# A hybrid decoder trunk on one core: the experts' up and gather products in four 32-column matmuls instead of one of 128

## The chip, the cores and the metric

The kernel runs on 1 core of one Trainium2 chip. The metric is the device time of one launch in microseconds (us); the kernel before takes 1231.05 us, the median of 3 runs (1229.32 to 1233.52).

## The reference, cut to what matters

Two layers over 256 tokens of 1024 features, all in float32. Each layer mixes the tokens in four groups of heads (sliding-window attention, gated linear attention, stick-breaking attention, RWKV-7), projects, adds, normalises, and applies a feed-forward part: dense in layer 0, and in layer 1 a mixture of 8 experts of which each token takes two. Only that mixture is touched by the change:

```python
def swiglu(h, w1, w3, w2):
    return (jax.nn.silu(h @ w1) * (h @ w3)) @ w2

def moe_swiglu(h, router, w1, w3, w2):
    logits = (h @ router).astype(F32)
    top_vals, top_idx = lax.top_k(logits, TOP_K)
    gates = jax.nn.softmax(top_vals, axis=-1)
    combine = jnp.sum(jax.nn.one_hot(top_idx, N_EXPERTS, dtype=F32) * gates[..., None], axis=-2)
    out = jnp.zeros_like(h)
    for e in range(N_EXPERTS):
        out = out + combine[..., e:e + 1].astype(h.dtype) * swiglu(h, w1[e], w3[e], w2[e])
    return out
```

w1 and w3 of an expert are 1024 x 1408, w2 is 1408 x 1024: 17.3 MB for each expert.

## The kernel before, in words

The kernel is written engine by engine (`build`, from line 196): one block of code for each of SyncE (SP, which issues the weight transfers), TensorE (`pe`), ScalarE (`act`), GpSimd and VectorE (`dve`). Each runs its own list in the order in which it is written; they meet through semaphores only: `full[b]` counts how often PSUM bank b was filled by TensorE, `free[b]` how often it was emptied. The order of the work is written by hand.

Layer 0 and the mixers of layer 1 come first. Then the function `experts` (called at the end of the `pe` block) does the mixture. The router picks experts; VectorE makes of the choice a one-hot matrix `pick` of 256 tokens x 96 slots (CAP = 96) for one expert. Then a loop of 8 passes runs on all engines (`Fori(0, n_passes * N_EXPERTS)`, where n_passes is 1 for these inputs), one pass per expert. One pass on TensorE is, in this order:

- **Up** (L1021 to L1035): 11 chunks of 128 hidden features. For each chunk and each of w1 and w3, 8 matmuls accumulate over the 1024 input features: the stationary operand is a 128x128 block of weights, the moving one the 96 gathered tokens (`slot_h`, in `region_m`). Chunks alternate between bank 0 and bank 1. After each chunk ScalarE applies silu (L1313) and VectorE multiplies (L1405, a helper), which frees the bank.
- **Transposes** (L1040) of the 96 weighing columns for this expert.
- **Gather** (`gather`, L994 to L1005) for the next expert: 8 feature blocks x 2 token tiles, the stationary operand a 128x128 block of normalised tokens in `tok`, the moving one `pick` with 96 columns, into banks 6 and 7. A first gather stands ahead of the loop.
- **Down** (L1047 to L1062): 22 matmuls of 512 columns whose stationary operand is 128 x 96 activations and whose moving one is w2, into banks 2 and 3 (96 partitions).
- **Scatter** (L1064 to L1069): 4 matmuls of 512 columns, `weigh_t` times `slot_y`, added to `x_sb` by VectorE.

All matmuls go through the helper `mm` (L517). Each float32 matmul of the program appears in the trace as two LDWEIGHTS (load of the stationary operand, PEld) and two MATMUL records; transposes (L522, L828, L1040) as one of each. One pass is 438 pairs of a load and a MATMUL: 352 in up, 2 transposes, 32 in the gather, 44 in down and 8 in the scatter.

SyncE loads each expert in 18 pieces (6 pairs of w1 and w3 columns, 6 pieces of w2; 1 MB each, the last of each kind half), into a ring of 9 slots, six in `ring` and three in `region_e`. Piece k + 9 is asked for when piece k has been used: for the up pieces the wait is on `full[0]` or `full[1]` after the second chunk of the pair.

Elsewhere the program has products on a part of the array: `GAT` in `b_scores` writes 64 partitions at a time, four matmuls of 64 weight columns and 256 moving columns, alternately to partitions 0 to 63 and 64 to 127 of one bank; `LW` and `LA` in `layer_mixers` contract over 64 rows, LW over rows 0 to 63, LA over rows 64 to 127, two matmuls each.

Of the kernel before, what the change touches and what calls it, by code (L numbers as in the profile page):

```python
# [11 lines left out]
AX_X = mybir.AxisListType.X  # L12

P = 128
D = 1024
KC = D // P
SEQ = 256
NT = SEQ // P
DEPTH = 2
# [12 lines left out]
D_FFE = 1408  # L32
UPC = D_FFE // P
UP2 = (UPC + 1) // 2
# [17 lines left out]
CAP = 96  # L52
# [31 lines left out]
def shape_constants():  # L84

    t = np.zeros((P, N_CONST), np.float32)
    i = np.arange(P)[:, None]
    j = np.arange(P)[None, :]

# [103 lines left out]
def build(nc, t_in, out):  # L193
    ctx = ExitStack()
    with ctx:
        def sb(name, shape, dt=F32):
            return ctx.enter_context(nc.sbuf_tensor(name, shape, dt))


        x_sb = sb("x_sb", [P, NT, D])  # L200
        tok = sb("tok", [P, NT, D])
        hT = sb("hT", [P, KC, SEQ])
# [21 lines left out]
        banks = [ctx.enter_context(nc.psum_tensor(f"bank{i}", [P, 512], F32)) for i in range(8)]  # L224
# [85 lines left out]
        slot_h = region_m[:, 0:KC * CAP].rearrange("p (c s) -> p c s", c=KC)  # L310
        pick = region_m[:, 768:768 + NT * CAP].rearrange("p (t s) -> p t s", t=NT)
        weigh = region_m[:, 960:960 + NT * CAP].rearrange("p (t s) -> p t s", t=NT)
        weigh_t = region_m[0:CAP, 1152:1152 + SEQ].rearrange("p (t n) -> p t n", t=NT)
        slot_y = region_m[0:CAP, 1408:1408 + D]
        place = region_m[:, 2432:2432 + NT * W].rearrange("p (t i) -> p t i", t=NT)
# [33 lines left out]
        def bank(name, l):  # L349
            return banks[uses[name, l][0]]  # L350
# [11 lines left out]
        def wait_open(pe, name, l):  # L362

            b, n = uses[name, l]
            if n:
                pe.wait_ge(free[b], n)
# [11 lines left out]
        def slot(n):  # L378
            return n % SLOTS
# [40 lines left out]
        def _(sp):  # L420
# [31 lines left out]
            for n, (what, l, at, m) in enumerate(pieces):  # L452
# [4 lines left out]
                elif n == 2:  # L457
                    sp.wait_ge(landed[slot(0)], 16)
                size = (KC if what in ("w_in", "w1", "w3") else D) * m
                dst = ring[:, slot(n), 0:size].rearrange("p (c n) -> p c n", n=m if size == KC * m and what not in ("w_out", "w2") else D)  # L460
                sp.dma_start(dst, source(what, l, at, m)).then_inc(landed[slot(n)], 16)
# [53 lines left out]
        def _(pe):  # L515
            def mm(o, lhsT, rhs, start=False, stop=False):
                return nc.tensor.matmul(o, lhsT, rhs, start=start, stop=stop, skip_group_check=True)  # L517
# [20 lines left out]
            def wait_features(names, l, k):  # L538

                if names and k % 2 == 0:  # L540
                    wait_evacuated(pe, names[k // 2], l)
# [432 lines left out]
            def experts(l):  # L974
                wait_open(pe, "RT", l)
                for t in range(NT):
                    for k in range(KC):
                        if t == 0:
                            wait_features(("F0", "F1", "F2", "F3"), l, k)
                        last = mm(bank("RT", l)[:, t * N_EXPERTS:(t + 1) * N_EXPERTS], hT[:, k, t * P:(t + 1) * P],  # L980
                                  router_sb[:, k, :], start=(t == 0 and k == 0), stop=(k == KC - 1))
                fills(last, "RT", l)


                pe.wait_ge(sem("chosen_ready"), 1)
                wait_open(pe, "POS", l)
                o = bank("POS", l)
                before, sel = const("upper")[:, 0:P], (chosen[:, 0, 0:N_EXPERTS], chosen[:, 1, 0:N_EXPERTS])
                mm(o[:, 0:8], before, sel[0], start=True, stop=True)
                mm(o[:, 8:16], const("all"), sel[0])  # L990
                mm(o[:, 8:16], before, sel[1], stop=True)
                mm(o[:, 16:24], const("all"), sel[0])
                fills(mm(o[:, 16:24], const("all"), sel[1], stop=True), "POS", l)

                def gather(b, waits):

                    for h in range(2):
                        if waits is not None:
                            pe.wait_ge(free[6 + h], waits[h])
                        for c in range(4):  # L1000
                            for t in range(NT):
                                last = mm(banks[6 + h][:, c * CAP:(c + 1) * CAP],
                                          tok[:, t, (4 * h + c) * P:(4 * h + c + 1) * P], pick[:, t, :],
                                          start=(c == 0 and t == 0), stop=(t == NT - 1))
                        last.then_inc(full[6 + h], 1)  # L1005

                pe.wait_ge(sem("picks"), 1)
                wait_open(pe, "G0", l)
                wait_open(pe, "G1", l)
                gather(0, None)  # L1010

                def landed_piece(i, k):
                    s, n = expert_landed(i, k)
                    pe.wait_ge(s, n)

                pe.wait_ge(sem("passes_ready"), 1)
                n_passes = pe.value_load(passes_i[0:1, 0:1], min_val=1, max_val=MAX_PASSES)
                with pe.Fori(0, n_passes * N_EXPERTS) as i:
                    pe.wait_ge(free[6], nth(i, 6, 0))
                    pe.wait_ge(free[7], nth(i, 7, 0))  # L1020
                    for p2 in range(UP2):  # L1021
                        m = min(256, D_FFE - 256 * p2)
                        landed_piece(i, 2 * p2)
                        landed_piece(i, 2 * p2 + 1)
                        w1 = expert_slot(2 * p2, KC * m).rearrange("p (c n) -> p c n", c=KC)
                        w3 = expert_slot(2 * p2 + 1, KC * m).rearrange("p (c n) -> p c n", c=KC)
                        for jj in range(m // P):
                            j = 2 * p2 + jj
                            b = j % 2
                            pe.wait_ge(free[b], nth(i, b, j // 2))  # L1030
                            for f, w in enumerate((w1, w3)):
                                for k in range(KC):
                                    last = mm(banks[b][:, f * CAP:(f + 1) * CAP], w[:, k, jj * P:(jj + 1) * P],
                                              slot_h[:, k, :], start=(f == 0 and k == 0), stop=(k == KC - 1))
                            last.then_inc(full[b], 1)  # L1035

                    pe.wait_ge(sem("weighs"), i + 1)
                    pe.wait_ge(free[2], nth(i, 2, 0))
                    for t in range(NT):
                        last = nc.tensor.transpose(banks[2][0:CAP, t * P:(t + 1) * P], weigh[:, t, :], ident)  # L1040
                    last.then_inc(full[2], 1)

                    pe.wait_ge(sem("picks"), i + 2)
                    gather(i, (nth(i, 6, 0), nth(i, 7, 0)))
                    pe.wait_ge(free[2], nth(i, 2, 1))
                    pe.wait_ge(free[3], nth(i, 3, 0))
                    for k2 in range(UP2):  # L1047
                        m = min(2, UPC - 2 * k2)
                        landed_piece(i, 2 * UP2 + k2)
                        w = expert_slot(2 * UP2 + k2, m * D).rearrange("p (c n) -> p c n", c=m)  # L1050
                        for kk in range(m):
                            j = 2 * k2 + kk
                            pe.wait_ge(free[j % 2], nth(i, j % 2, j // 2 + 1))
                        for half in range(2):
                            for kk in range(m):
                                k = 2 * k2 + kk
                                last = mm(banks[2 + half][0:CAP, :], slot_act[:, k, :],
                                          w[:, kk, half * 512:(half + 1) * 512], start=(k == 0), stop=(k == UPC - 1))
                            if k2 == UP2 - 1:
                                last.then_inc(full[2 + half], 1)  # L1060
                        if k2 < UP2 - 1:
                            last.then_inc(sem("moe_w2_used"), 1)  # L1062

                    for q, (b, t, half) in enumerate(SCATTER):  # L1064
                        pe.wait_ge(free[2 + half], nth(i, 2 + half, 2 - half))
                        if b > 3:
                            pe.wait_ge(free[b], nth(i, b, 0))
                        mm(banks[b][:, :], weigh_t[:, t, :], slot_y[:, half * 512:(half + 1) * 512],
                           start=True, stop=True).then_inc(full[b], 1)  # L1069
# [864 lines left out]
```

## Time and profile before

| | |
|---|---|
| median of 3 runs | 1231.05 us (1229.32 to 1233.52) |
| span of the profiled execution | 1229.1 us |
| the 8 passes of the expert loop | about 525 us of it |
| TensorE busy (MATMUL) | 1190.4 us, 97% |
| TensorE weight loads busy | 929.9 us, 76% |
| VectorE, ScalarE, GpSimd busy | 285.9, 192.3, 60.8 us |
| chain that ended last | TensorE 95%, VectorE 3% |
| transfers | 213.29 MB, mean 174 GB/s |

The span is measured from the first to the last instruction of that execution; no time of its own beside the span is recorded for the profiled execution, and the median of the runs is 1.95 us above it. How to read it: a MATMUL's duration holds its way through the array, so durations overlap, and what one costs in a row of them is the distance from one start to the next: the start of a group, its length and its count give it.

### The profile page before, as it was taken

Reading aid. Unit: us, or ns where it says so; the run is one execution under the profiler, and the core shown is the slowest. Engines: PE = TensorE matmul, PEld = TensorE weight load, DVE = VectorE, ACT = ScalarE, POOL = GpSimd, SP = SyncE. Lnnn points to the kernel's source line nnn. Section 1 sums busy time; section 2 is a strip of 40 time slices with the busy share of each in tenths; the row PEclk is TensorE's granted clock in tenths of the full one; section 3 lists DMA queues with packets and bytes.
Section 4 is the critical chain, followed back from the end, with each engine's and each line's share of the span. In section 5 each row is a group of like instructions: output and inputs, shape, how many; then the busy total and the mean of one; then the engine's idle time right before and its main releaser. Section 6 shows DMA issues by size and latency. Waiting matters only on the chain.

```text
span 1229.1 us, 16224 instructions
## 1 busy us (share of the span) xinstructions
PE 1190.4 (97%) x6686; PEld 929.9 (76%) x6686; DVE 285.9 (23%) x645; ACT 192.3 (16%) x444; POOL 60.8 (5%) x67
## 2 busy tenths in 40 slices
PE   7999999999999999999998899999999999999996
PEld 6886895688886448878884795959596978878692
DVE  4332663200000013143744201010110201010102
ACT  2243230200000002342221110010100101000011
POOL 2002221000000000004010000000000000000000
PEclk8999999899999999999999799999999999999998
DMA  9542102355445453432014378796969696878850
GB/s 326 166 137 69 35 2 70 100 172 169 137 137 196 146 154 120 139 103 69 1 35 152 108 269 259 257 306 227 305 204 318 214 306 219 301 232 289 253 205 34
DMA packets 168647, 213.29 MB, mean 174 GB/s; under 512 B 5120, under 2 KB 151200, under 8 KB 168480
## 3 DMA queue, kind: packets, MB, share of 16 engines
q1 hardware_dynamic: 166032, 210.29, 52.3%
q10 hardware_dynamic: 2576, 2.45, 0.7%
q8 instruction: 29, 0.48, 0.2%
q14 instruction: 10, 0.08, 0.0%
HBM read 211.67 MB, written 1.05 MB: 173 GB/s over the span
## 4 chain that ended last, share of the span: by engine, by line
PE 95%; DVE 3%; issue 1%; ACT 1%; POOL 0%; DMA 0%; DVEq 0%; POOLq 0%; ACTq 0%
PE bank L517 93%; PE bank L522 1%; DVE tok L1429 1%; POOL small L1338 0%; DMA x_sb<-in_x 0%; DVE b_att L1611 0%; DVE b_q L1408 0%; DVE x_sb L1405 0%; DVE region_m L1405 0%; PE bank L828 0%; ACT tok L1116 0%; DVE small L1420 0%; PE bank L1040 0%; ACT hT L1128 0%; PE bank L796 0%
## 5 line engine op out<-in xcount | busy, mean ns | idle before, releaser
L517 PE MATMUL bank<-hT,ring 128*128 128x256 f32 (+1 forms) x1184 | 261.8, 383 | 0.0
L517 PEld LDWEIGHTS bank<-hT,ring 128*128 128x128 f32 (+1 forms) x1184 | 224.4, 190 | 36.7 <-issue 2.9
L517 PEld LDWEIGHTS bank<-region_m,ring 128*128 128x128 f32 x2048 | 232.8, 193 | 5.1 <-issue 5.1
L517 PE MATMUL bank<-region_m,ring 128*128 128x96 f32 x2048 | 234.1, 276 | 1.6 <-DVE region_m L1855 1.6
L517 PE MATMUL bank<-ring,region_e 128*96 128x512 f32 (+1 forms) x368 | 159.4, 592 | 0.0
L517 PEld LDWEIGHTS bank<-ring,region_e 128*96 128x96 f32 (+1 forms) x368 | 64.1, 176 | 88.5 <-issue 88.5
L1405 DVE TENSOR_TENSOR region_e<-region_f,bank 128x96 f32<-128x96 f32 (+1 forms) x110 | 31.6, 287 | 424.4 <-ACT region_f L1313 279.8
L517 PE MATMUL bank<-ring,hT 128*128 128x256 f32 (+1 forms) x448 | 127.8, 442 | 1.4 <-ACT hT L1133 1.4
L517 PE MATMUL bank<-region_e 128*128 128x128 f32 (+2 forms) x512 | 117.7, 380 | 0.0
L517 PEld LDWEIGHTS bank<-ring,hT 128*128 128x128 f32 x448 | 84.0, 190 | 35.7 <-issue 25.8
L517 PEld LDWEIGHTS bank<-region_e 128*128 128x128 f32 (+1 forms) x512 | 70.4, 187 | 46.8 <-issue 46.7
L517 PE MATMUL bank<-region_m,region_e 128*128 128x96 f32 x768 | 88.4, 275 | 0.0
L517 PEld LDWEIGHTS bank<-region_m,region_e 128*128 128x128 f32 x768 | 87.0, 192 | 0.0
L1313 ACT ACTIVATE region_f<-bank 128x96 f32<-128x96 f32 x88 | 22.0, 250 | 315.5 <-PE bank L517 315.5
L1338 POOL TENSOR_TENSOR small<-small 128x1 f32<-128x1 f32 (+1 forms) x18 | 18.6, 1033 | 887.9 <-DVE small L1420 826.1
L1405 DVE TENSOR_TENSOR x_sb<-x_sb,bank 128x512 f32<-128x512 f32 x44 | 30.3, 688 | 93.5 <-PE bank L517 93.5
L517 PE MATMUL bank<-region_f 128*128 128x128 f32 (+1 forms) x352 | 43.0, 275 | 0.0
L517 PEld LDWEIGHTS bank<-region_f 128*128 128x128 f32 x352 | 41.2, 192 | 1.6 <-issue 1.6
L1875 DVE COPY region_m<-bank 96x512 f32<-96x512 f32 x8 | 5.5, 687 | 143.1 <-PE bank L517 143.1
L517 PE MATMUL bank<-region_m,tok 128*128 128x96 f32 x288 | 35.4, 284 | 1.2 <-DVE region_m L1778 1.2
L517 PEld LDWEIGHTS bank<-region_m,tok 128*128 128x128 f32 x288 | 34.8, 201 | 1.3 <-DVE region_m L1778 1.3
L522 PE MATMUL bank<-consts,tok 128*128 128x128 f32 x96 | 16.9, 325 | 14.1 <-DVE tok L1429 14.1
(234 smaller groups left out, 702.1 us busy)
## 6 DMA issues: line engine op xcount, KB each, us to landing
ring<-in_moe_w SPq DMA_DIRECT2D x80, 1024.0 KB, 6.0
region_e<-in_moe_w SPq DMA_DIRECT2D x40, 1024.0 KB, 5.7
ring<-in_ffn_w SPq DMA_DIRECT2D x33, 1024.0 KB, 5.4
ring<-in_w_in SPq DMA_DIRECT2D x22, 1024.0 KB, 5.3
ring<-in_w_out SPq DMA_DIRECT2D x8, 1024.0 KB, 4.9
ring<-in_moe_w SPq DMA_DIRECT2D x16, 512.0 KB, 5.3
region_e<-in_moe_w SPq DMA_DIRECT2D x8, 512.0 KB, 3.4
ring<-in_w_in SPq DMA_DIRECT2D x2, 1088.0 KB, 5.5
```

The source lines that it names most:

```text
L517: return nc.tensor.matmul(o, lhsT, rhs, start=start, stop=stop, skip_group_check=True)
L522: last = nc.tensor.transpose(bank(name, l)[:, cc * 256 + t * P:cc * 256 + t * P + P], tok[:, t, (2 * c2 + cc) * P:(2 * c2 + cc + 1) * P], ...
L1313: nc.scalar.activation(slot_silu[:, b, :], banks[b][:, 0:CAP], ACT.Silu).then_inc(sem("moe_silu"), 1)
L1338: g.tensor_tensor(ap_out, ap_in, m_half[:, 0:n], ALU.pow).then_inc(sem("rstd_ready"), 1)
L1405: return v.tensor_tensor(o, a, b, op)
L1429: v.tensor_scalar(tok[:, t, s], x_sb[:, t, s], scale, None, ALU.mult).then_inc(sem("h_ready"), 1)
L1875: v.tensor_copy(slot_y[:, 512:1024], banks[3][0:CAP, :]).then_inc(free[3], 1)
```

## The change

`HALF = 32` is a new constant. In the gather and in the up products, each matmul with 128 stationary columns and 128 output partitions becomes four, each with 32 stationary columns, which write partitions 0 to 31, 32 to 63, 64 to 95 and 96 to 127 of the same bank. The moving operand of all four is the same 96 columns. Nothing else changes; the new constant's line moves the lines behind it by one, the two new loops those behind them by more.

```diff
 P = 128
+HALF = 32
 D = 1024
...
                         for c in range(4):
                             for t in range(NT):
-                                last = mm(banks[6 + h][:, c * CAP:(c + 1) * CAP],
-                                          tok[:, t, (4 * h + c) * P:(4 * h + c + 1) * P], pick[:, t, :],
-                                          start=(c == 0 and t == 0), stop=(t == NT - 1))
+                                for q in range(0, P, HALF):
+                                    at = (4 * h + c) * P + q
+                                    last = mm(banks[6 + h][q:q + HALF, c * CAP:(c + 1) * CAP],
+                                              tok[:, t, at:at + HALF], pick[:, t, :],
+                                              start=(c == 0 and t == 0), stop=(t == NT - 1))
                         last.then_inc(full[6 + h], 1)
...
                             for f, w in enumerate((w1, w3)):
                                 for k in range(KC):
-                                    last = mm(banks[b][:, f * CAP:(f + 1) * CAP], w[:, k, jj * P:(jj + 1) * P],
-                                              slot_h[:, k, :], start=(f == 0 and k == 0), stop=(k == KC - 1))
+                                    for q in range(0, P, HALF):
+                                        at = jj * P + q
+                                        last = mm(banks[b][q:q + HALF, f * CAP:(f + 1) * CAP], w[:, k, at:at + HALF],
+                                                  slot_h[:, k, :], start=(f == 0 and k == 0), stop=(k == KC - 1))
                             last.then_inc(full[b], 1)
```

TensorE's list at the head of the loop, before: the wait for the two pieces, then one chunk, 16 matmuls into all 128 partitions (two trace pairs each).

```order
L1018 ISA
L1014 ISA
L1014 REGISTER_ALU
L1030 ISA
L517 MATMUL bank<-region_m,ring 128x96 x16
L1030 ISA
L517 MATMUL bank<-region_m,ring 128x96 x16
```

The same place in the changed kernel:

```order
L1021 ISA
L1017 ISA
L1017 REGISTER_ALU
L1033 ISA
L518 MATMUL bank<-region_m,ring 32x96 x64
L1033 ISA
L518 MATMUL bank<-region_m,ring 32x96 x64
```

A chunk is now 64 matmuls into 32 partitions each; the waits between chunks stay where they were.

The end of the pass, before: last chunk, transposes, gather, first part of down.

```order
L517 MATMUL bank<-region_m,ring 128x96 x16
L1037 REGISTER_ALU
L1038 ISA
L1040 MATMUL bank<-consts,region_m 96x128 x2
L1043 REGISTER_ALU
L517 MATMUL bank<-region_m,tok 128x96 x16
L1045 REGISTER_ALU
L1046 ISA
L517 MATMUL bank<-ring,region_e 96x512 x12
```

And in the changed kernel:

```order
L518 MATMUL bank<-region_m,ring 32x96 x64
L1042 REGISTER_ALU
L1043 ISA
L1045 MATMUL bank<-consts,region_m 96x128 x2
L1048 REGISTER_ALU
L518 MATMUL bank<-region_m,tok 32x96 x64
L1050 REGISTER_ALU
L1051 ISA
L518 MATMUL bank<-ring,region_e 96x512 x12
```

No instruction has changed its place; between two runs of 32-partition matmuls stand the transposes, and behind the gather the 96-partition matmuls of down.

## Rows read from the trace of the kernel before

**Rows 1.** The page: span, engines, and the chain by line.
```profile
span 1229.1 us, 16224 instructions
PE 1190.4 (97%) x6686; PEld 929.9 (76%) x6686; DVE 285.9 (23%) x645; ACT 192.3 (16%) x444; POOL 60.8 (5%) x67
PE 95%; DVE 3%; issue 1%; ACT 1%; POOL 0%; DMA 0%; DVEq 0%; POOLq 0%; ACTq 0%
```

**Rows 2.** The chain in order of time, pieces of the loop: start us, us, what.
```profile
734.00 65.41 PE bank L517 x436
...
865.25 65.40 PE bank L517 x436
...
1127.74 65.41 PE bank L517 x436
```

**Rows 3.** TensorE's timeline, one pass: start us, us, engine line op out<-in xcount.
```profile
825.59 21.58 PE L517 MATMUL bank<-region_m,ring 128*128 128x96 f32 x192
847.00 9.10 PE L517 MATMUL bank<-region_m,region_e 128*128 128x96 f32 x80
855.94 1.95 PE L517 MATMUL bank<-region_m,ring 128*128 128x96 f32 x16
857.72 1.95 PE L517 MATMUL bank<-region_m,region_e 128*128 128x96 f32 x16
859.51 5.52 PE L517 MATMUL bank<-region_m,ring 128*128 128x96 f32 x48
864.87 0.38 PE L1040 MATMUL bank<-consts,region_m 128*96 128x128 f32 x2
865.09 3.71 PE L517 MATMUL bank<-region_m,tok 128*128 128x96 f32 x32
...
887.57 3.80 PE L517 MATMUL bank<-region_m 96*128 96x512 f32 x8
```

**Rows 4.** The same view, long runs of 256 and of 512 moving columns.
```profile
239.83 60.38 PE L517 MATMUL bank<-hT,ring 128*128 128x256 f32 x279
...
385.50 64.97 PE L517 MATMUL bank<-ring,region_e 128*128 128x512 f32 x151
```

**Rows 5.** The timeline around GAT, then the durations and starts of its eight MATMULs.
```profile
133.72 0.44 PE L707 MATMUL bank<-consts,hT 128*128 128x128 f32 x2
134.09 0.63 PEld L517 LDWEIGHTS bank<-b_q,hT 128*64 128x64 f32 x8 [0.17 <-issue]
134.09 1.08 PE L517 MATMUL bank<-b_q,hT 128*64 128x256 f32 x8
135.10 0.60 PE L517 MATMUL bank<-region_e 128*128 128x128 f32 x3
...
L517 PE MATMUL bank<-b_q,hT x8: 379/379/431, 134.1 to 134.8; 128*64 128x256 f32 x8
...
134.09 0.14 PEld L517 LDWEIGHTS bank<-b_q,hT 128*64 128x64 f32 x2 [0.17 <-issue]
```

**Rows 6.** The timeline at LW (rows 0 to 63) and LA (64 to 127).
```profile
39.13 0.18 PEld L517 LDWEIGHTS bank<-region_m,lora 64*128 64x128 f32 x1 [0.33 <-issue]
...
39.15 0.18 PEld L517 LDWEIGHTS bank<-region_e,lora 64*128 64x128 f32 x1
```

**Rows 7.** Stretches: PE, PEld, DVE, ACT, POOL busy, PEclk, DMA share, GB/s.
```profile
762.00:769.00 7.00, 7.00 (x66) 7.00 (x64) 1.21 (x5) 0.50 (x2) 0.00 (x0) 1.00 0.15 43
...
804.00:811.00 7.00, 7.00 (x18) 2.64 (x17) 0.20 (x1) 0.00 (x0) 0.00 (x0) 1.00 1.02 312
...
825.60:891.20 65.60, 65.60 (x439) 51.59 (x438) 8.25 (x25) 5.98 (x18) 0.00 (x0) 1.00 0.79 264
```

**Rows 8.** Queues (packets, MB, share): whole page; 692 to 745 us; 745 us to 1193 us.
```profile
q8 instruction: 29, 0.48, 0.2%
...
q8 instruction: 4, 0.07, 0.5%
...
q14 instruction: 1, 0.01, 0.0%
```

**Rows 9.** Waits, 745 us to the end of the passes: waiter <- waited for: us, times, longest.
```profile
ACT region_f L1313 <- PE bank L517: 272.8, 76, 6.2
DVE region_e L1405 <- ACT region_f L1313: 238.5, 76, 3.3
```

**Rows 10.** The first gather, before the loop, and the stretch with its granted clock.
```profile
685.31 5.74 PE L517 MATMUL bank<-region_m,tok 128*128 128x96 f32 x32 [1.19 <-DVE region_m L1778]
...
681.00:689.00 8.00, 6.00 (x27) 5.90 (x28) 3.67 (x28) 0.31 (x2) 0.00 (x0) 0.50 0.01 2
```

**Rows 11.** Transfer issues of one pass: KB each, median us from issue to landing.
```profile
ring<-in_moe_w SPq DMA_DIRECT2D x10, 1024.0 KB, 6.0
```

## The prediction

> **What bounds the kernel now.** I read the page first: TensorE is busy for 97% of the span and has 95% of the chain that ended last; the chain knows no transfer to speak of [rows 1]. The chain in order of time then shows the loop of experts as eight equal pieces of 65.4 us, about 65.6 us from one to the next (734.00 to 1127.74 in six steps), unbroken TensorE work [rows 2]. So each nanosecond that a matmul of the loop gives back shortens the span, until something else is late. The loop is 525 us of the 1229.1.
>
> TensorE's timeline of one pass tells what a matmul costs there. From 825.59 to 859.51 stand 192 + 80 + 16 + 16 = 304 MATMULs of 96 moving columns, 33.92 us, so one starts every 111.6 ns [rows 3]. That is not the time in which 96 columns stream. Long runs of wider matmuls give that: 279 of 256 columns in 60.38 us are 216.4 ns each, 151 of 512 columns in 64.97 us are 430.3 ns each [rows 4]. The difference, 213.9 ns for 256 columns, is 0.836 ns a column, and 2.5 ns are left over for each matmul. For 96 columns this makes 80.2 + 2.5 = 82.7 ns. What takes 111.6 ns must be the load of 128 weight columns: at the same 0.836 ns a column it is 107 ns, plus 4.6. With 256 columns the load is hidden behind the stream, with 96 the stream is hidden behind the load. **Up and gather are bound by weight loads**, and the change cuts each load to a quarter, at the price of four times as many loads and four times as many streams. Everything hangs on whether the four streams run side by side.
>
> **Do parts of the array run side by side?** The kernel before has a place that shows it for halves. GAT's matmuls use 64 weight columns each and write alternately to the lower and the upper 64 partitions. Its eight MATMULs of 256 columns all start between 134.1 and 134.8 us and take 1.08 us from first start to last end [rows 5]; one after the other, their starts alone would be spread over 7 x 216 = 1.51 us. The first two loads lie in one piece of 0.14 us, which is the length of a single one [rows 5]. So two column tiles both load and stream at the same time, each at its full rate, though both belong to float32 matmuls and read all 128 rows. A second place shows that the queue lets work of another tile past: LW issues four loads and four MATMULs before LA's first load in program order, yet LA's first load starts at 39.15, 0.02 us behind LW's first [rows 6]. In the changed kernel the next tile's work stands only four instructions behind. Eight instructions in at most 0.03 us (by the two printed digits) are under 4 ns each; a group of four 32-column matmuls has four loads and four MATMULs per step of 82.7 ns, 10.3 ns each. Four tiles at once, and such a rate kept up for 30 us, no row shows.
>
> **The change part by part.**
>
> - *Up and gather in the loop.* Of each pass 352 + 32 = 384 pairs become 4 x 384. If four tiles stream side by side, a group of four starts every 82.7 ns in place of one every 111.6: 28.9 ns for each old pair, 11.1 us a pass, times 8: **-88.8 us**. A tile's own load, at 32 x 0.836 + 4.6 = 31.4 ns, hides behind its own stream of 82.7. The bounds of the group's period: 80.2 (no leftover at all) and 4 x 82.7 = 330.8 (no overlap at all). I take 82.7, by GAT, whose streams were not slowed by being two.
> - *The first gather.* It stands ahead of the loop, 32 pairs in 5.74 us, partly while the granted clock is 0.50, the 1.2 GHz level [rows 10]: 179 ns each. The same share, 26% of it, is **-1.5 us**.
> - *Going into small tiles and out again.* Around GAT: the transpose before it starts last at 133.72 + 0.44 - 0.27 = 133.89, and GAT at 134.09 where 0.11 later was due: 0.09 lost. Its last start is 134.8, 0.71 behind the first for three steps of two, where 0.65 was due: 0.06. The next matmul starts at 135.10, 0.30 later for 0.22: 0.08. The three behind take 0.60 with the last's 0.27 in it, 0.33 for two steps in place of 0.22: 0.11 [rows 5]. Together 0.34 us there and back. A pass does it twice (up, then the transposes, then the gather), the program 17 times: **+5.8 us**; nothing to double of that is the bound.
> - *Instruction fetches.* The trace has 29 of 0.48 MB in all, 16.5 KB each; four in the first pass, and in the seven others none but one small one of another queue [rows 8]: the loop is fetched once and stays. The program has (6686 - 7 x 438) x 2 = 7240 loads and MATMULs to fetch, so 66 bytes each. The loop grows from 876 to 2 x (1536 + 54) = 3180 of them, 0.21 MB or 13 fetches. Whether that much stays is not shown. If it does, nothing is added. If not, 13 fetches come back in every pass. One lasts 0.5% of 16 x 53 us / 4 = 1.06 us [rows 8], and a group of 256 instructions is used up in 2.6 us, so fetching ahead keeps up; straight code does so now without a gap (60.38 us of TensorE without an idle moment [rows 4]). What can show is the jump back, where nothing was fetched ahead: 1.06 us, behind scatter's 3.80 us of queued matmuls [rows 3]. Between 0 and two fetches a pass (17 us) I take half of one, since most of the first should be covered: **+4 us**. The Trainium skill, page "Runtime: NRT & Kernel Launch", section "Instruction fetch mechanics", gives TensorE's memory as 2048 instructions and says that a branch to a page which is not there waits for its fetch. By it the old loop fits and the new one does not, and these fetches will be seen; that no fetch stands in the seven later passes agrees for the old one.
> - *Everything else.* ScalarE waits 272.8 us for TensorE behind up chunks and VectorE 238.5 us for ScalarE [rows 9]; a chunk of 32 groups lasts 2.65 us in place of 3.57, two banks alternate, and both still wait. Nothing to add. Down and scatter are unchanged.
> - *The weights.* They hide behind TensorE; the cover shrinks from 65.6 to 65.6 - 11.1 + 0.7 = 55.2 us a pass. The transfers of a pass kept all engines busy for 0.79 of 65.6 us, 51.8 us [rows 7]. That still fits, with 3.4 us to spare. The share has been 1.02 over 7 us, and between bursts 0.15, when SyncE waited for a slot [rows 7]. Half a pass lies between asking and needing, against a median of 6.0 us to land [rows 11]. So 0, but it is the next thing to be late.
>
> Sum: -88.8 - 1.5 + 5.8 + 4 = -80.5 us, from the profiled 1229.1 to 1148.6. The runs shown lie 1.95 us above that execution in the median, so **1150.5 us**. This case's own range: 1136 (no leftover per matmul, 7.5 us; no fetch seen, 4; and some rounding) to 1167 (switches twice as dear, two fetches shown in each pass).
>
> **The rivals.**
>
> - *The weights become the bound.* For it: 51.8 us of transfers in a pass of 55.2 is 0.94 of all engines, which the old pass never sustained because of the waits for slots between bursts. Against: the lead of half a pass smooths bursts. At a share of 0.88 a pass lasts 58.9 us, 6.7 less than now: 8 x 6.7 = 54, so 1176.
> - *A floor on each matmul's issue.* GAT's pairs start within 0.01 us, but there were eight. If every MATMUL took 25 ns of issue, a group would take 100 ns, 11.6 less than now: 36 us less 10 for switches and fetches, 1205. The Trainium skill states just this number: page "TensorE: Matmul & The Clock Gate", section "Wait — 56ns, not 53.3ns?", says that start-to-start never falls below about 25 ns however few the columns. By that rule the sum would be 1205 and not 1150; starts of two tiles in one 0.14 us piece [rows 5] speak for counting it per tile.
> - *Instructions come too slowly*, the case on the other side. If the 13 fetches of a pass were not fetched ahead, each would stop TensorE for 1.06 us: 104 of them cost 110 us, more than the 90.3 gained, so 1231 - 90 + 6 + 110 = 1257. It decides from 0.8 us shown per fetch. Against it: straight code hides them now, at a slower use.
> - *Loads of different tiles queue for one path.* Then a group takes 4 x 31.4 = 125.6 ns, or 117 if only 2.5 ns are lost per load, against 111.6 now: 1258 to 1285. The one pair of loads in 0.14 us speaks against it.
> - *Only two tiles stream at a time.* All that the trace shows is two. A group then takes 2 x 82.7 = 165.4 ns, 53.8 more than now, on 3104 old pairs: +167, with switches and fetches 1408.
>
> **How the numbers follow.** Chances: the forecast 0.62, weights 0.10, issue floor 0.07, instructions 0.05, loads in line 0.06, two at a time 0.10. About 0.3%, 3.7 us, is what a measurement can tell from no change. Faster: 0.62 + 0.10 + 0.07 = 0.79, of which I move 0.01 to no change, where a mixture of cases could land; slower 0.21. Up to 1210 the cases hold under 0.79, less the tails of the first; so the range goes on to 1260, which takes in the instructions and the cheaper end of the loads: 1136 to 1260.
>
> **What would show it.** Right: TensorE's timeline with 128 MATMULs of 32x96 every 2.65 us, passes 55 to 56 us apart in the chain, SyncE waiting less, DMA share near 0.93. The weights: TensorE idle ahead of a piece, released by a transfer. The issue floor: passes near 62 us with TensorE never waiting. Fetches: 13 packets of the instruction queue in each pass, and TensorE idle at the head of the loop. Two at a time or loads in line: passes of 86 or 68 us, the starts of the four tiles spread over 165 or 117 ns. The forecast is wrong if a pass is longer than 58 us.

## The result and the profile after

| | before | after |
|---|---|---|
| median of 4 runs | 1230.18 us (1228.49 to 1233.52) | 1363.45 us (1354.62 to 1367.33) |
| span of the profiled execution | 1229.1 us | 1365.5 us |
| mean granted clock of TensorE | 0.982 | 0.939 |
| ratio of the times | | 1.1071, 95% interval 1.1035 to 1.1108 |

The change makes the kernel 10.7% slower, 133 us; 1150.5 us was forecast. The page of the changed kernel: span, busy time, the granted clock in 40 slices, the instruction queue, the chain by engine, and the groups of the 32-column matmuls.

```profile
span 1365.5 us, 34848 instructions
PE 1170.9 (86%) x15998; PEld 888.0 (65%) x15998; DVE 285.9 (21%) x645; ACT 192.9 (14%) x444; POOL 60.9 (4%) x67
PEclk9999999999999999999889999899998889989898
q8 instruction: 137, 2.24, 0.7%
PE 84%; issue 12%; DVE 2%; ACT 1%; POOL 0%; DMA 0%; DVEq 0%; POOLq 0%; ACTq 0%
L518 PE MATMUL bank<-region_m,ring 128*32 128x96 f32 x8192 | 224.1, 276 | 89.1 <-issue 87.5
L518 PE MATMUL bank<-region_m,region_e 128*32 128x96 f32 x3072 | 83.5, 266 | 52.2 <-issue 52.2
L518 PE MATMUL bank<-region_m,tok 128*32 128x96 f32 x1152 | 30.5, 265 | 17.2 <-issue 16.0
```

TensorE was busy for 97% and had 95% of the chain [rows 1]; now it is busy for 86%, and 12% of the chain is "issue": the engine had nothing to run and waited for nothing that the profile shows. No DMA and no other engine took its place. The loss stands ahead of the new matmuls (89.1 + 52.2 + 17.2 us). The packets of the instruction queue went from 29 [rows 8] to 137.

The chain in order of time, one pass in the middle of the loop (start us, us, what), says where:

```profile
998.43 24.97 PE bank L518 x149
1023.40 3.09 issue
...
1029.53 10.46 PE bank L518 x382
1039.98 3.29 issue
1043.28 7.13 PE bank L518 x254
1050.41 2.50 issue
1052.91 2.84 PE bank L518 x127
1056.76 2.85 PE bank L518 x127
1059.60 3.83 issue
1063.43 10.53 PE bank L518 x381
...
1082.80 24.97 PE bank L518 x149
```

Before, this was one piece of 65.4 us [rows 2]. Now 84.4 us lie from one down product (998.43) to the next (1082.80). In between are bursts of about 127, or two or three times that, and pauses of 2 to 4 us. 128 MATMULs with their loads are 256 instructions. By the page a packet of the instruction queue is 2.24 MB / 137 = 16.4 KB, and at the 66 bytes each of the prediction that is about 250 instructions: **one packet, one burst**. The first piece, 24.97 us, is down, scatter and the first matmuls of the next pass; then follows the pause at the jump back, 3.09 us here and 3.2 and 3.7 in its neighbours. The queues in 520 us of the loop:

```profile
q1 hardware_dynamic: 86251, 105.53, 61.7%
q8 instruction: 86, 1.41, 1.1%
```

Before, seven of the eight passes had none of these packets [rows 8]. In the records of the trace 111 stand behind the loop's start, 14 a pass, 3.0 us apart at the least, 4.3 in the median, up to 7.6 in up and gather; one lasts 1.05 us.

The jump itself is on record as an instruction of TensorE's queue. Here it is before and after: the shortest, the median and the longest duration in ns, of eight (the shortest, the last pass's, jumps nowhere).

```profile
L1018 PEldq COMPARE_BRANCH  x8: 76/208/248, 757.5 to 1216.8; - x8
L1021 PEldq COMPARE_BRANCH  x8: 83/5612/7128, 765.9 to 1353.2; - x8
```

Where the loop is fetched anew, the jump takes 5.2 to 7.1 us in place of 0.2. The next packet of the instruction queue starts 2.7 to 4.6 us behind the jump's start and lasts 1.1 us, and the jump ends some 1.4 us behind it. So one fetch that is waited for takes over 5 us, of which the packet is one; scatter's queued matmuls cover part of it.

Inside a burst the array did what was forecast: 127 MATMULs end after 2.84 us, and the last one's 0.24 us taken off, this is 82 to 83 ns for each group of four (82.7 forecast). Often the four tiles of a group start 7 ns apart; elsewhere they are out of step, at the same 82 to 83 ns a group.

The granted clock adds its share. Two stretches of 10 us (busy us of PE, PEld, DVE, ACT, POOL; then PEclk, DMA share, GB/s):

```profile
860.00:870.00 10.00, 9.10 (x296) 8.76 (x292) 0.51 (x2) 0.50 (x2) 0.00 (x0) 0.65 0.01 3
890.00:900.00 10.00, 6.42 (x289) 5.77 (x280) 0.76 (x3) 0.72 (x3) 0.00 (x0) 1.00 0.93 363
```

At 890 TensorE is idle for a third of the time at full clock, and as many MATMULs (289 against 296) are done as at 860, where it is busy for 91% at a mean clock of 0.65. Over the loop the clock stands at 0.50, the 1.2 GHz level, for 126 us; before it was 3.4 us. A group of four takes 160 ns there, so a stretch at half clock eats up part of the time in which the next block arrives; clock and pauses can't simply be added.

### The profile page after: what moved, and what is told of

Read it like the earlier page. It is cut to its first block, busy times and chain, and to the rows that moved or that the text cites. A ratio compares the mean times of both kernels' runs of the same rounds, so it can differ in the third digit from the quotient of the medians.

```text
span 1365.5 us, 34848 instructions
## 1 busy us (share of the span) xinstructions
PE 1170.9 (86%) x15998; PEld 888.0 (65%) x15998; DVE 285.9 (21%) x645; ACT 192.9 (14%) x444; POOL 60.9 (4%) x67
## 3 DMA queue, kind: packets, MB, share of 16 engines
q8 instruction: 137, 2.24, 0.7%
HBM read 211.67 MB, written 1.05 MB: 156 GB/s over the span
## 4 chain that ended last, share of the span: by engine, by line
PE 84%; issue 12%; DVE 2%; ACT 1%; POOL 0%; DMA 0%; DVEq 0%; POOLq 0%; ACTq 0%
PE bank L518 82%; PE bank L523 1%; DVE tok L1434 1%; POOL small L1343 0%; DMA x_sb<-in_x 0%; DVE b_att L1616 0%; DVE b_q L1413 0%; PE bank L1045 0%; DVE x_sb L1410 0%; DVE region_m L1410 0%; PE bank L829 0%; ACT tok L1121 0%; DVE small L1425 0%; ACT hT L1133 0%; PE bank L797 0%
## 5 line engine op out<-in xcount | busy, mean ns | idle before, releaser
L518 PE MATMUL bank<-region_m,ring 128*32 128x96 f32 x8192 | 224.1, 276 | 89.1 <-issue 87.5
L518 PEld LDWEIGHTS bank<-region_m,ring 128*32 128x32 f32 x8192 | 211.2, 126 | 103.6 <-issue 103.5
L518 PE MATMUL bank<-region_m,region_e 128*32 128x96 f32 x3072 | 83.5, 266 | 52.2 <-issue 52.2
L518 PEld LDWEIGHTS bank<-region_m,region_e 128*32 128x32 f32 x3072 | 76.1, 121 | 57.4 <-issue 57.4
L518 PE MATMUL bank<-region_m,tok 128*32 128x96 f32 x1152 | 30.5, 265 | 17.2 <-issue 16.0
L518 PEld LDWEIGHTS bank<-region_m,tok 128*32 128x32 f32 x1152 | 27.0, 119 | 20.4 <-issue 19.1
L518 PE MATMUL bank<-region_m 96*128 96x512 f32 x64 | 30.4, 617 | 0.0
```

## The experiments

Two readings stood against each other. **A, supply**: the loop has grown from 919 to 3223 instructions (loads, MATMULs and 43 others), no longer stays with the engine and is fetched anew in every pass, more slowly than it is used up. **B, the array**: four narrow tiles cost something in themselves, say in the clock, and the fetches only go along. A loop "stays" if passes behind the first bring no packets of the instruction queue. A block is 256 instructions, about what one packet holds. Each ratio is to the kernel before, run beside the experiment on the same chip.

**Half the instructions, nearly the same gain on the array.** `e1_two64` changes one number of the changed kernel:

```diff
-HALF = 32
+HALF = 64
```

> Up and gather in two matmuls of 64 weight columns in place of four of 32. Theory (the instruction supply is what failed: the loop of 3180 loads and MATMULs no longer stays and its blocks of 256 come slower than they are used): here the loop has 2 x (768 + 54) = 1644. If that stays, two tiles side by side give the same period of 82.7 ns as four, no instruction fetch after the first pass, and the sum of the prediction without its fetch term: 1229.1 - 88.8 - 1.5 + 5.8 + 2 = about 1147 us. If 1644 do not stay, fetches come back, 6 or 7 a pass, but a block then lasts 5.3 us of streaming, so 1150 to 1180. Rival (small column tiles themselves stall the engine, whatever the instructions): slower than before, 1260 to 1300 by half of the loss.

Measured 1143.84 us (1141.67 to 1145.25), ratio 0.9298 (0.9272 to 0.9325). The chain in order of time:

```profile
943.05 54.73 PE bank L518 x820
997.78 0.35 PE bank L1045 x2
998.13 54.73 PE bank L518 x820
```

The passes are unbroken again and last 55.08 us, where the forecast for the changed kernel had 55.2. Behind 745 us the instruction queue of TensorE has no packet at all. The expectation was about 1147. So two tiles side by side give what the sum said; B in its plain form ("split products don't pay") is gone.

**Four tiles, few instructions.** `e2_gather32` undoes the split of up and keeps that of the gather:

```diff
+                            n = P
...
-                                    for q in range(0, P, HALF):
+                                    for q in range(0, P, n):
...
-                                        last = mm(banks[b][q:q + HALF, f * CAP:(f + 1) * CAP], w[:, k, at:at + HALF],
+                                        last = mm(banks[b][q:q + n, f * CAP:(f + 1) * CAP], w[:, k, at:at + n],
```

> Only the gather in four matmuls of 32 columns, up as before. Theory: 2 x 534 = 1068 instructions in the loop stay resident, no fetch after the first pass; 9 gathers of 32 pairs gain 28.9 ns each, 8.3 us, less 9 x 0.34 = 3.1 for going into small tiles and out: about 5 us faster than before, 1225 us. Rival (four tiles stall by themselves): each gather longer than 3.7 us, so slower than before by 5 us or more.

Measured 1223.59 us (1220.99 to 1224.4), ratio 0.9948 (0.993 to 0.9967): 6.4 us gained, about as expected (1225). Four narrow tiles are no loss where the loop (1111 instructions) stays: 4 packets behind its start, all in the first pass.

**How long may the loop be?** `e3_up32_5` and `e5_up32_4` leave the gather whole and split the first 5 or 4 of the 11 chunks of up into four; the edit of the second:

```diff
+                            n = HALF if j < 4 else P
...
-                                    for q in range(0, P, HALF):
+                                    for q in range(0, P, n):
```

> Up in four matmuls of 32 columns for chunks 0 to 4 of 11, the other chunks and the gather as before: 2 x (438 + 480) = 1836 loads and MATMULs in the loop. Theory (supply) with a memory of some 2000 instructions: stays, 160 old pairs a pass gain 28.9 ns, 37 us in all, less 8 x 0.34 = 2.7: about 1196 us, and no fetches after the first pass. If 1836 do not stay: the five chunks use a block in 2.65 us and get one in 3.5 or more, 1233 to 1330 us. Rival (four tiles stall by themselves): 5/11 of the change's loss, about 1290 us, without fetches.

> As the run with five chunks in four matmuls of 32 columns, but with four chunks: 2 x 822 = 1644 loads and MATMULs in the loop, as many as in the version with 64 columns, which stayed; five chunks (1836) did not stay and took 1309 us. Theory (only the loop's length decides): stays, no fetch after the first pass, 128 old pairs a pass gain 28.9 ns, 8 x 3.7 = 29.6 us, less 2.7 for the tiles' switches: about 1202 us, four tiles at 82 ns a group. Rival (four narrow tiles cannot be fed even out of the engine's memory): 4/5 of the loss of five chunks, about 1290 us.

Measured 1309.48 us (1295.52 to 1317.0), ratio 1.0587 (1.0519 to 1.0655), and 1298.18 us (1296.06 to 1300.9), ratio 1.0546 (1.0502 to 1.059). Both lose, with 78 and 70 packets behind the loop's start. The first lies in its second case (the loop does not stay: 1233 to 1330). The second is a miss, about 1202 expected, and taught most: its loop has 1687 instructions, exactly as many as that of `e1_two64`, which stays. Its chain:

```profile
956.29 26.12 PE bank L518 x84
982.41 3.93 issue
...
989.35 6.96 PE bank L518 x254
996.31 0.71 issue
997.02 2.85 PE bank L518 x128
999.87 3.85 issue
1003.72 30.60 PE bank L518 x342
```

The gaps stand at the jump and in the split chunks; none is in the 7 whole chunks (in the piece of 30.60), where a block lasts 14 us. So length alone does not decide whether a loop stays.

**Is it the weights' transfers?** `e4_thin_weights` is the changed kernel with hardly any traffic beside the fetches. It leaves out most of each expert's weights, so its results are not the program's; TensorE's list of instructions is the same:

```diff
-                sp.dma_start(dst, src).then_inc(expert_landed(e, k)[0], 16)
+                sp.dma_start(dst[:, 0:1, 0:128], src[:, 0:1, 0:128]).then_inc(expert_landed(e, k)[0], 16)
```

`e4b_thin_before` is the same edit in the kernel before, as a control.

> The changed kernel, but each transfer of an expert piece brings only 128 columns of its first row block, so the experts are computed with weights that are mostly not theirs: the queues are nearly empty in the loop, everything else as in the change. If instruction blocks come late because they queue behind weight packets: blocks come closer together than 3.5 us, the gaps of TensorE go, and the time falls towards 1150 to 1200 us. If a block's time is a round trip of its own: smallest distance of 3.5 us as before, packets of about 1 us, and the time within 2% of the changed kernel, 1335 to 1365 us.

> Control for the run with thin transfers: the kernel before with each transfer of an expert piece bringing only 128 columns of its first row block, so the experts are computed with weights that are mostly not theirs. Theory: its instructions stay in the engine's memory and no transfer was waited for, so the time is that of the kernel before, 1229 us within 0.5%. Rival: the weight transfers slow TensorE by themselves (its reads, its clock); then it is faster, and so much of the 114 us that the thin transfers gave the changed kernel is not the fetches'.

Measured 1249.08 us, ratio 1.016 (1.0125 to 1.0195), and 1230.64 us, ratio 1.0005 (0.9981 to 1.0029). The control doesn't move: before, the transfers cost TensorE nothing. In the changed kernel they cost 114 us. The first lies between its two expectations (1150 to 1200, or 1335 to 1365): each named half of the cause. Its chain, in up:

```profile
906.29 2.85 PE bank L518 x128
...
920.17 2.84 PE bank L518 x127
923.01 0.82 issue
923.83 2.84 PE bank L518 x127
926.67 0.93 issue
927.60 2.85 PE bank L518 x128
```

and a stretch of 10 us of it, with the columns as above:

```profile
900.00:910.00 10.00, 7.96 (x366) 7.31 (x360) 0.76 (x3) 0.75 (x3) 0.00 (x0) 1.00 0.06 18
```

There are as many packets as in the changed kernel, 111, but they come every 3.55 us in the median and never under 3.0, and the pauses shrink to about 1 us. With DMA idle for 94% of the time a block still takes more than the 2.65 us in which it is used up. The jump back shows the fetch by itself again (ns, as above):

```profile
L1021 PEldq COMPARE_BRANCH  x8: 82/3536/3802, 754.2 to 1235.1; - x8
```

It takes 3.4 to 3.8 us. The packet starts 0.9 to 1.5 us behind the jump's start, in place of 2.7 to 4.6, lasts about 1.1 us as before, and the jump ends 1.4 us behind it as before. So the weights' transfers put off the packet's start and hardly lengthen the packet. The clock is at 0.50 for 17 us of the loop. Supply with almost no traffic beside it costs 1249.08 - 1143.84 = 105 us; the transfers stretch the median distance to 4.3 us, and this, with the falls of the clock in and behind the longer pauses, makes the other 114. How the 114 divide between the two was not measured, nor why the packets of this kernel keep 3.0 us apart.

**Fetching anew, with wide matmuls.** `e6_unroll4` writes TensorE's loop of the kernel before out, four passes to a turn, so that it can't stay:

```diff
-                with pe.Fori(0, n_passes * N_EXPERTS) as i:
+                with pe.Fori(0, n_passes * (N_EXPERTS // 4)) as i4:
+                  for u in range(4):
+                    i = i4 * 4 + u
```

> The kernel before, only TensorE's loop written out four passes at a time (2 turns): 2 x 1752 = 3504 loads and MATMULs in the loop, more than the changed kernel's 3180, none narrower than before. Theory: it does not stay, about 14 fetches of 256 instructions for every four passes, but each block now lasts 14 us of TensorE work against 3.5 us or more between two fetches, so all are hidden; only the one jump back may show 3 to 4 us less what scatter covers: 1229 to 1234 us, no change. Rival (any loop that does not stay costs by its fetches): 14 more fetches at about 1.5 us each, 1250 us or more.

Measured 1237.47 us (1235.28 to 1241.68), ratio 1.0061 (1.004 to 1.0082). The queue from 745 to 1200 us, and the chain around the one jump back:

```profile
q8 instruction: 27, 0.44, 0.4%
...
929.41 26.12 PE bank L517 x84
955.54 3.39 issue
958.93 43.79 PE bank L517 x352
```

32 packets come behind the loop's start, mostly 14 us apart, and all but the jump's are hidden. The time lies 3.5 us above the expected 1229 to 1234, and the one jump explains it: the pass with the jump lasts 73.6 us where the others last 65.6, 3.39 of the 8 being the pause and the rest behind it, where the clock is at 0.50 for 10 us. Being fetched costs 0.6%, 7.5 us, here. What costs 133 is being fetched *and* used up in 2.65 us.

**Does the place in memory decide?** In blocks of 256 instructions, counted from the program's first and set by where the fetches fall in the trace, the loop of `e5_up32_4` lies at 25.91 to 32.50, that of `e1_two64` at 26.16 to 32.75. `e9_up32_4_moved` shifts the former by 60 instructions that do nothing of use, behind the warm-up:

```diff
+            for _ in range(15):
+                mm(banks[5][:, 0:2], hT[:, 0, 0:P], hT[:, 0, 0:2], start=True, stop=True)
```

> The version with four chunks in 32 columns took 1298 us, with 1687 instructions in the loop, as many as the fast version with 64 columns; its loop lies over blocks 25.91 to 32.50 of 256 instructions, counted from where the fetches fall, which touches 8 blocks, while the fast one lies over 26.16 to 32.75 and touches 7. Here 15 small matmuls (2 moving columns) are added behind the warm-up, 60 instructions, so the loop lies over 26.14 to 32.73. Theory (7 blocks stay, 8 don't): no fetch after the first pass, four tiles at 82 ns a group, 1202 us and up to 2 us for the added matmuls. Rival (narrow tiles cannot be fed, or only the count matters): 1298 us.

Measured 1208.92 us (1208.53 to 1212.9), ratio 0.9834 (0.9803 to 0.9866): **89 us less, for instructions added**. Its chain is whole again:

```profile
922.04 0.22 PE bank L1046 x2
922.25 62.01 PE bank L518 x820
```

Four tiles side by side over 4 chunks, 10.6 us at a time, run unbroken when the loop stays. This settles B. Some 5 us are left to the expected 1202 to 1204. They lie in the first pass, which is still fetched: it lasts 7.5 us longer than the others from its first MATMUL to its scatter, where the kernel before has 1.7.

**More products in two tiles.** `e8_more64` adds to `e1_two64` the attention outputs of the mixers, whose matmuls are also narrower in what moves than in what is loaded, through a helper:

```diff
+            def mm2(o, lhsT, rhs, start=False, stop=False):
+                for q in (0, 64):
+                    last = mm(o[q:q + 64], lhsT[:, q:q + 64], rhs, start=start, stop=stop)
+                return last
```

`e10_more64_moved` is the same with 19 of the small matmuls, 76 instructions.

> Up and gather with 64 columns, and in the mixers also the products of 64 moving columns (CO, the first part of GO, AO, Y0, Y1) in two column tiles of 64. These are bound by a load of 128 columns, 112 ns a pair; two tiles of 64 would start every 58 (64 x 0.836 + 4.6). 24 + 16 + 24 + 16 + 24 = 104 pairs a layer gain 54 ns, 5.6 us a layer, less four times 0.34 for going there and back (GO's second part is in such tiles already): 4.3 a layer, 8.5 us in all if all of it lies on the chain: 1135 to 1144 us. Rival: waits on other engines take it up, 1144 us.

> The version with more products of 64 columns took 1185 us; its extra 416 instructions ahead of the loop push the loop to 27.78 to 34.37, over 8 blocks. Here 19 small matmuls (76 instructions) move it to 28.08 to 34.67, over 7. Theory: no fetches after the first pass, and what the mixers gain shows: 1135 to 1142 us, faster than the version with 64 columns in up and gather alone (1143.8). Rival: the mixers' small tiles themselves cost the 41 us: 1185 us.

Measured 1185.1 us (1183.7 to 1189.16), ratio 0.9627 (0.9596 to 0.9657), and 1138.51 us (1135.06 to 1141.03), ratio 0.9252 (0.9224 to 0.9279). The first is a miss (1135 to 1144 expected). The loop is the one of `e1_two64`, but instructions put ahead of it had moved it to 27.78 to 34.37; it was fetched in every pass (70 packets), with a pause of 3.3 to 5.0 us at each jump. At four of the seven jumps the first two packets stand only 1.1 to 1.5 us apart, so 3.0 us is not the least the queue can do. Moved on to 28.08 it stays, in passes of 55.1 us. `e10_more64_moved` is the fastest version found and beats both kernels.

**The same loop in two more places.** `e11_two64_moved` and `e12_two64_place5` are `e1_two64` with 22 and with 48 of the small matmuls:

> The fast version (up and gather in 64 columns, 1143.8 us), with 22 small matmuls (88 instructions) behind the warm-up and nothing else: the loop moves from 26.16 to 32.75 to 26.50 to 33.09 and touches 8 blocks. Theory: it no longer stays, 8 fetches a pass come back with the gap at the jump, 1180 to 1190 us as in the version with more products in 64 columns. Rival (the place of the loop does not matter): 1144 us and at most 5 for the added matmuls.

> The kernel of e1_two64 (up and gather in two matmuls of 64 columns, a loop of 1687 instructions) with 48 small matmuls (192 instructions) behind the warm-up, in place of the 22 of e11_two64_moved. Counted in blocks of 256 instructions the loop then lies at 26.91 to 33.50: the same place within a block, and the same length, as in e5_up32_4, where it did not stay, while at 26.16 to 32.75 and at 26.50 to 33.09 it stayed. Theory A: eight blocks can stay, and the fetching runs one block ahead of the one in use once that is used beyond its first part, so a loop that ends well inside its eighth block (.50 here, .37 and .50 in e8 and e5) loses its first block and then all; at .09 (e11) it doesn't. Then fetches come back in every pass, some 60 to 75 behind the loop's start, gaps of 3 to 6 us at each jump, and a time of 1175 to 1200 us. Theory B: the place within a block does not decide, something else in e5 and e8 did (the mixture of wide and narrow matmuls, the other products' instructions): then it stays, 5 to 6 fetches, passes of 55.1 us, 1146 to 1155 us.

The first is a miss: measured 1151.96 us (1146.14 to 1158.92), ratio 0.938 (0.9331 to 0.9429), 6 packets behind the loop's start, passes of 55.1 us. The loop stays, though by the count it touches eight blocks. Two of its four runs took 1146 us and two some 1158; the profile is of one at 1146, so what the other two did is not known. The second run hit Theory A of its expectation in kind, and cost more than that said: 1213.74 us (1212.3 to 1214.56), ratio 0.988 (0.9861 to 0.9898). Its queue from 745 to 1180 us and its chain:

```profile
q8 instruction: 62, 1.02, 1.0%
...
923.27 25.54 PE bank L518 x116
948.81 4.40 issue
...
956.10 31.62 PE bank L518 x692
```

The loop of `e1_two64`, instruction for instruction, takes 70 us more 192 instructions further on. The pauses of a pass make 5 to 6 us; the rest goes with the clock, which is at 0.50 for 61 us of the loop, and at no time in the loop of `e1_two64`. All cases together (the place is counted, not read):

| run | loop's instructions | place in blocks | stays |
|---|---|---|---|
| before; e2_gather32 | 919; 1111 | 25.91 to 29.50; 26.66 to 31.00 | yes |
| e1, e9, e10 | 1687 | 26.16 to 32.75; 26.14 to 32.73; 28.08 to 34.67 | yes |
| e11 | 1687 | 26.50 to 33.09 | yes |
| e8, e5, e12 | 1687 | 27.78 to 34.37; 25.91 to 32.50; 26.91 to 33.50 | no |
| e3_up32_5 | 1879 | 25.91 to 33.25 | no |
| after | 3223 | 26.66 to 39.25 | no |

One reading fits all of them: there is room for eight blocks, and fetching runs ahead into the next once the one in use is past its first part. A loop that ends well inside its eighth block then loses its first. The packets agree: `e5_up32_4` and `e12_two64_place5` touch eight blocks and bring nine packets a pass. The reading was formed before `e12_two64_place5` and forecast that it would not stay, but it was fitted to the other rows; where between .09 and .37 of the last block the border lies was not tried. The Trainium skill, page "Runtime: NRT & Kernel Launch", section "Instruction fetch mechanics", gives 2048 instructions, which is eight blocks of 256, with the next page fetched while the current one runs: the runs agree with that size. The same section calls the cost of crossing a block mostly hidden; that holds for blocks that last 14 us (`e6_unroll4`) and fails for blocks that last 2.65 us.

## Why the prediction was wrong

- **What bounds the kernel, right.** TensorE's work in the loop, bound by weight loads. Wherever the loop stayed in an experiment, the time followed the sum made from it: `e1_two64`, `e2_gather32`, `e9_up32_4_moved`, `e10_more64_moved`.
- **Up and gather, -88.8 us, right on the array.** 82 to 83 ns for a group of four against 82.7 forecast. The doubt, "four tiles at once, and such a rate kept up for 30 us, no row shows", was well placed, but the rate was limited elsewhere: the four tiles ran side by side for 10.6 us in `e9_up32_4_moved` with nothing between them. Thirty unbroken microseconds of them no run shows; the one loop with so many did not stay.
- **Going into small tiles and out, +5.8 us, right.** Passes that stay are steady enough to read it. From the old 65.62 us, 28.9 ns off for each split pair gives 64.70 in `e2_gather32`, 61.92 in `e9_up32_4_moved` and 54.52 in `e1_two64`; measured are 65.02, 62.22 and 55.08. That is 0.32 and 0.30 us for one time there and back and 0.56 for two, against 0.34 for one.
- **Instruction fetches, +4 us: the step that failed.** That the loop might not stay was seen, and the 13 fetches of a pass were counted nearly rightly (there are 14). The failing sentence is: "One lasts 0.5% of 16 x 53 us / 4 = 1.06 us, and a group of 256 instructions is used up in 2.6 us, so fetching ahead keeps up". The packet's duration was right (1.05 us), but it is neither the distance of two fetches nor the time that one takes: in this kernel packets never came closer than 3.0 us, with 3.55 in the median with DMA almost idle and 4.3 with the weights running, and the fetch at the jump took 5.2 to 7.1 us. In place of +4 us the fetches cost 105 us, and 220 with the weights' traffic and the clock. The row that was leant on, straight code without an idle moment [rows 4], has blocks that last longer than that: 128 MATMULs at 216.4 ns are 27.7 us. It could not tell 1 us from 4.
- **Everything else and the weights, 0 us: right where the loop stays**, 55.08 us a pass with no wait for a transfer, though the weights' queue takes 94.1% of the DMA engines in the loop of `e1_two64`, as 51.8 of 55.2 us had said. In the changed kernel the transfers did cost time, not by arriving late (DMA has 0% of the chain) but by slowing the fetches: a collision that the prediction did not look for.
- **The rivals.** The case on the other side, "instructions come too slowly", was the right one, at a chance of 0.05, and mis-sized: 104 fetches at 1.06 us each gave 1257. The rule was wrong in form: a pause is the distance of the fetches less the use of a block, and one at the jump comes on top. With 3.55 and 2.65 us, 12 such pauses and 1.5 us at the jump this makes 12.3 us a pass for `e4_thin_weights`, whose passes are 13.8 us longer than those of `e1_two64`. The likeness of 1249 in `e4_thin_weights` to its 1257 is chance. Weights as the bound, the floor of 25 ns (four MATMULs start 7 ns apart and the next four 82 ns later, so if there is one it holds for a tile at most), loads in line and two at a time all fell.
- **The size.** 1363.45 - 1150.5 = 213 us. Two tiles in place of four gave 1143.84, 6.7 under the forecast; supply without traffic adds 105, the weights' transfers and the clock 114: -6.7 + 105 + 114 = 213. That this sum closes is no proof of its first part, as `e1_two64` stands in for four tiles in a loop that stays.

## What to carry to other kernels

A narrower tile multiplies instructions, so ahead of it, divide the block of 256 instructions by the rate at which TensorE will use them up: of the loops that did not stay here, blocks of 2.65 us were bound by their fetches, blocks of 5.3 us (`e8_more64`, `e12_two64_place5`) showed them at the jump and mostly not beyond the block behind it, and blocks of 14 us at the jump alone. Heavy DMA traffic beside the fetches makes it worse. Split no further than needed: two tiles of 64 columns gave 7.0% here, with half the instructions of the four that lost 10.7%. And when a loop of some 1700 instructions changes its speed after an edit elsewhere, look at the instruction queue in its later passes and at the duration of its jump, and try it 60 to 80 instructions further on.

## What the runs showed of the hardware that was not expected

- The same loop takes 1143.84 or 1213.74 us with its place as the only difference (192 instructions that do nothing of use), and 1298.18 or 1208.92 us with 60 of them.
- Packets of the instruction queue last 1.05 us; in the changed kernel they come at least 3.0 us apart, and with the expert weights moving, at a DMA share of 61.7% in the loop, 4.3 us in the median. In `e8_more64` two stood 1.1 us apart at a jump.
- The jump back takes 0.2 us where the loop stays; where it doesn't, 3.4 to 3.8 us with DMA almost idle and 5.1 to 7.2 us with the weights moving. Behind 3.8 us of scatter that were queued, TensorE then stands still for 1.2 to 1.7 us and for 2.9 to 5.0 us.
- Two column tiles of float32 hold 55.08 us a pass; four can start 7 ns apart, and end a group every 82 to 83 ns.
- In and behind the pauses the granted clock fell to 0.50 again and again: for 126 us of the loop in the changed kernel, 17 us where the pauses were about 1 us long, 3.4 us in the kernel before and none in `e1_two64`, whose passes are unbroken.
